# Out-projection, norm, feed-forward and second norm as one block in a two-layer encoder

## What is computed

```python
for layer in range(DEPTH):
    m = s5_mixer(h, ...) if kind == 0 else hgrn2_mixer(h, ...)   # both end in "... @ w_out"
    h = layer_norm(DEEPNORM_ALPHA * h + m, ln_mix_g[layer], ln_mix_b[layer])
    f = swiglu(h, ffn_w_in[layer], ffn_w_out[layer])             # (silu(gate) * up) @ w_out, hidden 2816
    h = layer_norm(DEEPNORM_ALPHA * h + f, ln_ffn_g[layer], ln_ffn_b[layer])
```

## Time and profile before

| | us |
|---|---|
| median of 3 runs | 3101.9 (3097.56 to 3102.55) |
| profiled execution | 3100.69 |
| its span in the trace | 3098.9 |
| TensorE busy | 2786.3 (90%) |
| VectorE busy | 1449.8 (47%) |
| GpSimd busy | 707.2 (23%) |
| ScalarE busy | 591.7 (19%) |

### The profile page before, as it was taken

One profiled execution on the slowest core, in us unless ns is written; L12 is line 12 of the kernel. 1 busy time (PEld: TensorE's weight loads), 2 busy tenths in 40 slices (PEclk: granted clock), 3 DMA queues, 4 the chain that ended last, 5 costly groups with the idle time before them and its releaser, 6 DMA issues. The chain is left out here.

```text
span 3098.9 us, 37027 instructions
## 1 busy us (share of the span) xinstructions
PE 2786.3 (90%) x14372; PEld 2343.9 (76%) x14372; DVE 1449.8 (47%) x2392; ACT 591.7 (19%) x849; POOL 707.2 (23%) x489
## 2 busy tenths in 40 slices
PE   6685789699999999968999999998778999999994
PEld 5574668588888888757888888888557888888884
DVE  8588422642332323364555655555745323233326
ACT  3223231211111111041222222220311111111111
POOL 3777321321112111111111111110421121111212
PEclk8887889799999999979999999996789999999997
DMA  4232220311111110031001011000312111111101
GB/s 137 67 107 86 70 82 41 95 55 41 54 41 41 55 53 27 0 95 35 28 21 34 20 34 34 27 7 1 122 41 82 41 54 54 41 54 41 41 14 68
DMA packets 213107, 157.96 MB, mean 51 GB/s; under 512 B 21792, under 2 KB 196000, under 8 KB 211872
## 3 DMA queue, kind: packets, MB, share of 16 engines
q1 hardware_dynamic: 213024, 156.83, 16.8%
HBM read 139.04 MB, written 17.76 MB: 51 GB/s over the span
## 5 line engine op out<-in xcount | busy, mean ns | idle before, releaser
L468 PE MATMUL ps<-aT_hi,ffn_w_hi 128*128 128x512 f32 x1408 | 556.0, 395 | 18.0 <-PEq L238 18.0
L468 PE MATMUL ps<-aT_hi,ffn_w_lo 128*128 128x512 f32 x1408 | 552.3, 392 | 0.0
L468 PE MATMUL ps<-aT_lo,ffn_w_hi 128*128 128x512 f32 x1408 | 548.4, 389 | 0.0
L551 DVE TENSOR_TENSOR ffn_act_out<-ffn_act_out,ps 128x512 f32<-128x512 f32 x88 | 60.5, 688 | 710.6 <-ACT ffn_act_out L523 710.6
L568 DVE TENSOR_TENSOR h<-h,ps 128x512 f32<-128x512 f32 x352 | 241.9, 687 | 216.0 <-PE ps L482 213.9
L468 PEld LDWEIGHTS ps<-aT_hi,ffn_w_hi 128*128 128x128 f32 x1408 | 265.4, 189 | 72.7 <-issue 18.7
L616 POOL CAST ffn_hid_hi<-ffn_act_out 128x512 fp32r<-128x512 f32 x88 | 57.6, 655 | 1114.5 <-PE ps L482 584.3
L468 PEld LDWEIGHTS ps<-aT_hi,ffn_w_lo 128*128 128x128 f32 x1408 | 264.8, 188 | 61.9
L468 PEld LDWEIGHTS ps<-aT_lo,ffn_w_hi 128*128 128x128 f32 x1408 | 265.2, 188 | 58.6
L482 PE MATMUL ps<-ffn_w_hi,ffn_hid_hi 128*128 128x512 f32 x704 | 276.5, 393 | 6.8 <-POOL ffn_hid_lo L619 6.8
L482 PE MATMUL ps<-ffn_w_hi,ffn_hid_lo 128*128 128x512 f32 x704 | 275.7, 392 | 0.0
(11 more groups left out here) (257 smaller groups left out, 4285.3 us busy)
## 6 DMA issues: line engine op xcount, KB each, us to landing
ffn_w_raw<-in_ffn_w_in_dram SPq DMA_DIRECT2D x88, 512.0 KB, 5.1
ffn_w_raw<-in_ffn_w_out_dram SPq DMA_DIRECT2D x22, 1024.0 KB, 5.0
hg_w_raw<-in_hg_w_in_dram SPq DMA_DIRECT2D x40, 512.0 KB, 3.9
h<-in_x_dram SPq DMA_DIRECT2D x4, 1024.0 KB, 8.9
s_w_raw<-in_s_w_in_dram SPq DMA_DIRECT2D x8, 512.0 KB, 4.5
s_scratch_u<-h SPq DMA_DIRECT2D x16, 256.0 KB, 2.4
s_u_grp<-s_scratch_u SPq DMA_DIRECT2D x64, 64.0 KB, 2.2
s_pw_in<-s_scratch_kern SPq DMA_DIRECT2D x64, 64.0 KB, 2.5
```

The lines of the kernel that those rows point to most:

```text
L468: ins = t.matmul(ps[:, 2 * b + a, :], w[q][:, a, kk, :], x[:, kk, rows], start=(kk == 0 and m == 0), stop=(kk == KT - 1 and m == 2))
L551: v.tensor_tensor(act_out[u % 2][:, :], act_out[u % 2][:, :], ps[:, 2 * (u % 2) + 1, :], ALU.mult).then_inc(s_prod, 1)
```

## The change

A new function, `project_and_feed`, holds out-projection, first norm, feed-forward and second norm in one block and is called twice. The old functions only note their arguments; `layer_norm_block` and `final_norm_block` call it. In layer 0 it gets the first weights of the recurrence and the place to spill to, in layer 1 the output (`turns` is false there).

- Buffers: three raw buffers of 1 MB (`raw0` to `raw2`), and eight split buffers (four high, four low) are shared by the weights of the projection, of the feed-forward, and by the hidden tile. The projection's weights come in four pieces of 1 MB (column half, four slices); the fourth waits until the first four slices are split. Feed-forward weights are loaded as soon as pieces are split. `raw0`, `hi0` and `lo0` outlive the block, and the first weights of the recurrence are views of them.
- The projection's first column half goes slice by slice, with the eight token tiles in the eight banks. Low parts of its weights are made by VectorE. The second half goes by token tiles as before, in four banks. The residual is scaled by `ALPHA` in the sum from PSUM, in both layers; the spilled tiles now have scale and shift.
- The norm works on two token tiles at a time (`normalise`), with three refinement steps (`NEWTON`), and two operations a tile with `g` and `b` as rows. A pair is turned (`turn`) behind the second-half products of the next pair, the last one behind the first product unit. ScalarE takes the high part and VectorE the low part straight from PSUM (`keep_turned`).
- In the feed-forward the first group's sum from PSUM scales the residual. The last group's units are ordered so that token half 0 comes first (`SPLIT`); the outputs of tiles 0 to 3 follow it, then units 2 and 3 with the transposes of tiles 0 to 3 between (in layer 0), then the outputs of tiles 4 to 7. Each pair is normed as its sums end, and stored.
- Tokens lie in the order "tile, then partition" between the blocks now, not "partition, then tile", so the strided view of the split moves from the recurrence's side to that of S5 (`cut`).
- In the scan, for group 1, `inputs(3)` and `turn_bl(2)` come ahead of the output of group 0, and `keep_y(0)` behind `place_c(2)`; two waits are adapted.

The diff, cut to its core:

```diff
+NEWTON = 3
+PIECE = 2 * D
+def project_and_feed(k, gamma_out, beta_out, first_weights=(), spill=None, out=None):
+    raw = [k.raw0, sb("raw1", [P, PIECE]), sb("raw2", [P, PIECE])]
+    hi1, lo1, w2h, w2l, hidh, hidl = (sb(n, [P, PIECE], F32R) for n in (...))
+    proj_hi = [[k.hi0, w2h], [hi1, hidh]]
+    proj_lo = [[k.lo0, w2l], [lo1, hidl]]
+    PLAIN, SPLIT = [(0, 0), (0, 1), (1, 0), (1, 1)], [(0, 0), (1, 0), (0, 1), (1, 1)]
...
+        # sync
+            for dh in range(2):
+                for kh in range(2):
+                    if 2 * dh + kh == 3:
+                        load_rows(gamma_mid, beta_mid)
+                    load_piece(dh, kh)
+            s.wait_ge(S["x_lo"], KT)
+            for half in range(2):
+                tiles = slice(4 * half, 4 * half + 4)
+                s.dma_start(h[:, tiles, :], residual_v[:, tiles, :]).then_inc(S[f"back{half}"], 16)
+            s.wait_ge(S["w_lo"], 8)
+            load_w1(0, 1)
+            s.wait_ge(S["w_lo"], 12)
+            load_w2(0)
+            s.wait_ge(S["w_lo"], 16)
+            load_w1(0, 0)
...
+        # tensor
+            for kk in range(KT):
+                t.wait_ge(S["x_lo"], kk + 1)
+                t.wait_ge(S["w_lo"], kk + 1)
+                for tt in range(NT):
+                    ins = project(0, kk, tt, tt)
+            for pair in range(PAIRS):
+                second_half(2 * pair)
+                second_half(2 * pair + 1)
+                if pair >= 1:
+                    turn(2 * pair - 2, 2 * pair - 2)
+                    turn(2 * pair - 1, 2 * pair - 1)
+            unit(0, 0)
+            turn(NT - 2, NT - 2)
+            turn(NT - 1, NT - 1)
+            group(0)
+            with t.Fori(1, NG - 2) as i:
+                group(i)
+            group(NG - 2)
+            unit(LAST, 1)
+            outputs(LAST, slice(0, 4), 2)
+            unit(LAST, 2)
+            if turns:
+                turn(NT, 0)
+                turn(NT + 1, 1)
+            unit(LAST, 3)
+            if turns:
+                turn(NT + 2, 2)
+                turn(NT + 3, 3)
+            outputs(LAST, slice(4, NT), 4)
+            if turns:
+                for tt in range(4, NT):
+                    turn(NT + tt, tt)
...
+        # vector
+            def add_projection(dh, tt):
+                v.scalar_tensor_tensor(part, part, ALPHA, ps[:, tt if dh == 0 else tt % 4, :], ALU.mult, ALU.add)
+                v.bn_stats(k.stats[:, tt, dh, :], part)
+            def normalise(pair, first_stat, rows, spent):
+                for _ in range(NEWTON): ...
+                for n, tt in enumerate((2 * pair, 2 * pair + 1)):
+                    v.scalar_tensor_tensor(h[:, tt, :], h[:, tt, :], mv[:, tt, 0:1], g_row[:, :], ALU.subtract, ALU.mult)
+                    v.scalar_tensor_tensor(h[:, tt, :], h[:, tt, :], rstd[:, tt:tt + 1], b_row[:, :], ALU.mult, ALU.add)
+            for tt in range(NT):
+                add_projection(0, tt)
+            for pair in range(PAIRS):
+                for tt in (2 * pair, 2 * pair + 1):
+                    add_projection(1, tt)
+                normalise(pair, NT + 2 * pair + 2, 1, pair)
+                if pair >= 1:
+                    keep_turned(2 * pair - 2, 2 * pair - 2)
+                    keep_turned(2 * pair - 1, 2 * pair - 1)
...
+        # gpsimd
+            split_w2(0)
+            split_w1(0)
+            split_w1(1)
+            hidden(0, 0)
...
 # s5_scan_block, tensor
-                        if n >= 3:
+                        if n >= 4:
                             t.wait_ge(S["y_kept"], 2 * (n - 2))
-                if n + 2 < KT:
+                if n == 0:
+                    t.wait_ge(S["u_kept"], 2 * 4)
+                elif n + 2 < KT:
                     t.wait_ge(S["u_kept"], 2 * (n + 3))
                 make_kern(n)
+                if n == 1:
+                    inputs(n + 2, (0, 1))
+                    turn_bl(n + 1)
                 within_chunks(n - 1)
                 across_chunks(n - 1)
-                if n + 2 < KT:
+                if 2 <= n < KT - 2:
                     inputs(n + 2, (0, 1))
-                if n + 1 < KT:
+                if 2 <= n < KT - 1:
                     turn_bl(n + 1)
 # s5_scan_block, scalar
-                keep_y(n - 1)
+                if n >= 2:
+                    keep_y(n - 1)
...
+                if n == 1:
+                    keep_y(0)
```

More of the change, by code:

```diff
@@ new lines, in unit @@
+            def unit(i, pos):
+                q, half = units(i)[pos]
+                b = pos % 2
+                if half == 0 and (pos == 0 or q):
+                    t.wait_ge(S[f"w1_lo{q}"], i + 1)
+                if isinstance(i, int) and i == 0 and pos < 2:
+                    t.wait_ge(S["acc"], NT + 6 + 2 * pos)
+                    t.wait_ge(S["lo"], 8 if half == 0 else 2 * NT)
+                else:
+                    t.wait_ge(S["prod"], i * U + pos - 1)
+                rows = slice(half * HALF, (half + 1) * HALF)
@@ L472, in outputs @@
-            def outputs(i):
-                t.wait_ge(s_hl, (i + 1) * U)
-                if not (isinstance(i, int) and i == 0):
-                    t.wait_ge(s_w2l, i)
-                for m in range(NOUT):
+                ins.then_inc(S["unit"], 1)
+            def outputs(i, tiles, hidden):
+                t.wait_ge(S["hid"], i * U + hidden)
+                t.wait_ge(S["w2_lo"], i + 1)
+                for m in range(2 * tiles.start, 2 * tiles.stop):
                     tt, dh = m // 2, m % 2
@@ L517, in silu @@
[L517 to L525 removed]
+                if isinstance(i, int) and i == 0:
+                    a.wait_ge(S["tile"], (q + 1) * NT)
+                else:
+                    a.wait_ge(S["unit"], (i - 1) * U + 2 * q + 2)
+                    carry(a, i)
@@ new lines, in product, with accumulate @@
+            def product(i, pos):
+                b = pos % 2
+                v.wait_ge(S["silu"], i * U + pos + 1)
+                v.tensor_tensor(act_out[b][:, :], act_out[b][:, :], ps[:, 2 * b + 1, :], ALU.mult
+                                ).then_inc(S["prod"], 1)
+            def accumulate(i, tiles, last=False):
+                first = isinstance(i, int) and i == 0
+                if not first and tiles.start == 0:
+                    v.wait_ge(S["out_acc"], i * NOUT)
+                for m in range(2 * tiles.start, 2 * tiles.stop):
@@ L589, in group @@
-                accumulate(i, last=not more)
-            product(0, 0)
-            v.wait_ge(rows_ready, 1)
-            affine(range(3))
-            group(0, True, start=True)
-            with v.Fori(1, NG - 1) as i:
-                group(i, True)
-            group(NG - 1, False)
+                split_w1(i + 1, 1)
+                product(i + 1, 0)
+                accumulate(i, slice(0, NT))
+            group(0)
+            with v.Fori(1, NG - 2) as i:
+                group(i)
+            group(NG - 2)
@@ L599, in _ @@
+            if turns:
+                for tt in range(4, NT):
+                    keep_turned(NT + tt, tt)
         @block.gpsimd
```

775 lines of the change are left out of this document (313 added, 462 removed).

## The result

The changed kernel takes 2989.02 us (median of 4 runs, 2987.38 to 2990.9), the kernel before 3102.0 beside it: a ratio of 0.9642, with a 95% interval of 0.963 to 0.9653. The forecast was 2995, with 2978 to 3025 as its range. The span of the profiled execution is 113.3 us shorter, 3098.9 to 2985.6, where the sum of the prediction was 106.2.

A forecast was written before the change was run, and what follows sets the result against it. TensorE was taken to bound feed-forwards and recurrence, leaving gains between stages: 42.6 + 47.6 + 11 + 8 - 3 = 106.2 us. From 3100.69 that gives 2994.5, with 1.2 for the median 2995.7, say 2995; range 2978 to 3025.

The forecast's parts named there:

- What bounds the kernel: TensorE stays busy through feed-forwards and recurrence; time can be won in four places between those stages.
- The start of A and C: Out-projections of layers 0 and 1: first product 6.5 us after the weight load's issue, first half ends at 53.6.
- The second half: Out-projection's second half with norms under it, both layers: 57 us from the first half's end, with TensorE hardly waiting.
- Stage B: End of feed-forward 0 up to the recurrence: 91.4 us becomes 79.4, gain 12.0, taken as 11, bounds 6 and 14.
- The recurrence: Between the layers, behind feed-forward 0: no term in the sum, forecast gain 0.
- Stage D: End of feed-forward 1 to the run's end: 84.1 us becomes 75.9, gain 8.2, taken as 8, bounds 5 and 10.
- The scan stage: Reordered scan: group 2 waits for the output's trip, stage ends 2.7 us later; 3 lost taken, bounds 2 gained, 6 lost.
- Rival 1: VectorE becomes the bound in the norms at all four places, costing 39 us, so 3034 us; chance 0.11.
- A cold first half: Out-projection's first half runs at the lower granted clock, near 0.5; chance 0.03.
- Rival 3: Feed-forward loops: shared buffers make groups wait for weights, slower than before, 3155 us at 8 us per group; chance 0.03.
- Rival 4: Out-projections: norms run after the second half, only the starts gain, some 25 us in all, 3077 us; chance 0.03.

The follow-up runs named there:

- scan_order: Changed kernel with the scan stage's order as before (fourth input product and group 1 transposes behind group 0's output): 2985.37 us, ratio 0.9629.
- newton6: Changed kernel with six refinement steps of the reciprocal root instead of three: 3012.34 us, ratio 0.9717.
- tile_order: Changed kernel with the first column half of both out-projections walked token tile by token tile instead of slice by slice: 3012.33 us, ratio 0.9723.
- norm_after: Changed kernel with the first norms of both layers behind all second-half products of the out-projection instead of under them: 3037.19 us, ratio 0.9798.
- plain_last: Changed kernel with the last group of both feed-forwards ordered like the others, all four units before the outputs: 3013.31 us, ratio 0.972.
- pool_low: Changed kernel with low parts of the out-projection's first column half made by GpSimd instead of VectorE: 2991.51 us, ratio 0.9648.
- late_split: Changed kernel with GpSimd's third weight split of the first group waiting until all eight tiles are normed: 2985.87 us, ratio 0.963.
- all: Changed kernel with the scan order as before, GpSimd's third split late and two refinement steps instead of three: 2982.26 us, ratio 0.9621.

## Why the prediction held, point by point

- What bounds the kernel: held. The loops took 679.8 and 679.9 us in both kernels, to 0.1; the whole gain lies in the four places between the stages.
- The start of A and C: held. 6.54 and 6.62 us to the first product (6.5), 53.96 and 52.88 to the second half (53.6). The landing of 5.0 was right in effect: ScalarE's first split started 5.04 us after the issue in layer 0. The prices for a cold start (2.3, in other sums 1.4 and 2.1, and 1.3 at the feed-forward starts of before) were my estimates, and no run shows any of them as one price: over 44.8, the two first halves took 2.6 and 1.5 more (47.42 and 46.26 us); over 11.0, the scan's 48 products took 0.8 more (105.70 to 117.46); and the feed-forward starts of before took 1.4 and 1.5 more (from the first product to the first output 56.37 and 56.45 us, where five units are 54.95).
- The second half: held in its queue, with one step wrong in form. Unit 0 started at 49.98 (50.5), unit 1 at 67.8 (65.4). I spread GpSimd's disturbance over four operations of 1.04 each (2.25 instead of 1.21), 4.2 us; it was one of 4.25 (5.53 instead of 1.28), a lock. The sum was nearly the same, and its place too: the stage after the first half came to 58.3 in A and 56.2 in C. The 2.1 between them are the clock behind the last wait, which the 57 did not price.
- Stage B: 78.2, where the working gave 79.4 and I took a gain of 11 instead of 12. In the working, the term that was mis-sized is the restart of the first outputs. I charged 2.1 us for the lower clock; behind the same wait of 3.42 us as before they started at 0.49 and took 11.03 us for 48 products, the 10.9 without the charge. In layer 1 the charge was due: behind the same wait they started at 0.79 and took 13.71 us.
- The recurrence: the missing term, 2.9 us. I ended the sum at its first product and gave that start no clock. Before, it came after 13.42 us of waiting and at the lower clock (0.77 for the first product); after the change it follows the last transposes by 1.68 us (1313.40) and starts at 0.47. In the first 26 us (before, then after):

```profile
1365.40:1391.40 26.00, 25.94 (x103) 21.17 (x104) 1.55 (x3) 6.15 (x11) 2.41 (x1) 0.90 0.33 79
...
1313.30:1339.30 26.00, 25.90 (x113) 21.32 (x114) 1.54 (x3) 7.98 (x12) 2.81 (x2) 1.00 0.33 79
```

103 products and a granted clock of 0.90 against 113 and 1.00.
- Stage D: 75.1, forecast 75.9 by its working.
- The scan stage: held in its sign and its queue, the one part of the change that is a loss. Forecast 3; 2.1 in this profile, and from the kernel products to group 2 1.9 more than in the kernel before and 2.7 more than in scan_order. Group 2 itself came 1.1 us later in the span (142.54 after 141.39), not 2 to 3: the output stood at 129.08 (129.2), but the trip behind it took 13.5 us, not 14.7.
- Rival 1 (VectorE the bound): not so here, but by less than the prediction thought, 0.2 us a pair. newton6 is that rival made true.
- A cold first half (0.03 of the chances): no. In the first 5.65 us, from 449.65, the granted clock was 0.50; from 455.3 on, through the eight banks in turn, it was the full one (busy time of the stretch, columns as above):

```profile
455.30:497.00 41.70, 41.70 (x180) 33.46 (x179) 23.65 (x27) 15.16 (x18) 0.00 (x0) 1.00 0.60 203
```

TensorE was busy for 41.70 of the 41.70 us. In tile_order, which also has the eight banks but whose first tile follows the splits, the granted clock was 0.50 in the stretch shown, with 8.99 busy of 10.00 us.
- Rival 3 (stalls in the loops): no, by the loops' lengths. Rival 4 (no overlap): norm_after and plain_last show what it would have cost, 72 us of the gain.

So the sum was 7.1 us short: 2.9 in the recurrence, 2.2 in B, 1.8 in C, 1.0 in D and 0.9 in the scan stage, less 1.6 too much in A. Of B's 2.2, 1.0 is the gain of 12 taken as 11. The recurrence and the rest of B are restarts that came out at the higher clock; the prediction had one row for such a restart, and left the recurrence's out. Two slips in its numbers change nothing: by the earlier trace rows the trip of the scan's output is 14.9 us, not 14.7 (128.16 + 5.23 + 2.2 - 120.70), and its chance of 0.80 stands beside two ranges, up to 3018 and up to 3025.

## What to carry to other kernels

A gain between stages is read as two queues run against each other from a common zero; that gave each of eight marks to within 2.4 us here. What it misses is the clock at each restart, so every wait that the change shortens or moves, the first one of the next stage too, belongs in the range with 2 to 3 us (2.7 here: 48 products in 13.71 us behind one wait, in 11.03 behind another). And a product order that needs only one slice at a time makes it nearly irrelevant who prepares the slices, as long as a slice's splits take less time than its products (5.6 us), as they did in pool_low.

## What the hardware showed that I had not expected

- The same wait, two clocks. TensorE waited 3.42 us for the hidden tile in both layers of the changed kernel, behind the same units. At 1238.62 it restarted at the higher clock (48 products in 11.03 us), at 2913.89 at the lower (13.71 us). Each came out alike in the second profile of the same kernel (0.50 and 0.79). In the other kernels it came out either way: in layer 0, at the higher clock at 1235.82 in late_split (0.50 for the first product, after 3.42 us of waiting) and at the lower at 1233.96 in all (0.79, after 3.43). What decides it, no run here shows.
- In two places the clock fell behind the restart, not at it: in late_split's layer 1, after a wait of 2.04 us, about 1 us after a start at full speed, for 3.3 us (products 0.43 us apart instead of 0.23), and in scan_order's layer 0, after a wait of 3.42 us, about 1.4 us after the start at 1233.75, for as long.
- VectorE and GpSimd locked each other out for whole operations where VectorE's read two tiles of SBUF: 5.53 us for a VectorE operation of 1.28, and 13.66 for a GpSimd operation of 1.27 while VectorE's queue had no gap. A sum that read PSUM and one tile kept its 0.67 us beside a split of 4.63.
